# PEER down loop on one Trainium2 core: one product of 512 columns for two of 256, sums in eight banks

## What is computed

```
h   = gelu(tokens @ u.T)              # a value for each token and each expert
G   = summed softmax weights of the picked experts, 0 elsewhere
out = (h * G) @ v                     # 16384 experts, D = 1024
x   = x + gate * out
```

## Time and profile before

| | us |
|---|---|
| median of 3 runs | 4567.59 |
| lowest and highest run | 4564.38, 4571.7 |
| profiled execution, its own time | 4573.89 |
| profiled execution, span of its instructions | 4571.8 |
| TensorE busy | 4217.0 (92%) |
| TensorE weight loads busy | 3981.0 (87%) |
| VectorE busy | 3068.6 (67%) |
| ScalarE busy | 1813.9 (40%) |

### The profile page before, as it was taken

One profiled execution on the slowest core, in us unless ns is written; L12 is line 12 of the kernel. 1 busy time (PEld: TensorE's weight loads), 2 busy tenths in 40 slices (PEclk: granted clock), 3 DMA queues, 4 the chain that ended last, 5 costly groups with the idle time before them and its releaser, 6 DMA issues. The chain is left out here.

```text
span 4571.8 us, 87598 instructions
## 1 busy us (share of the span) xinstructions
PE 4217.0 (92%) x33409; PEld 3981.0 (87%) x33418; DVE 3068.6 (67%) x5237; ACT 1813.9 (40%) x2655; POOL 37.9 (1%) x54
## 2 busy tenths in 40 slices
PE   8978999969888589999999899999988889999998
PEld 8956999859784489899999898999987589899998
DVE  5565565555523648887777598877772659887777
ACT  4324343333322434444333444443332444444333
POOL 0000000000000001000000010000000001000000
PEclk9988999989899899999999999999999999999999
DMA  6633666526420037555776575567752157556775
GB/s 233 203 118 108 228 201 230 165 75 227 152 94 19 29 124 229 181 177 184 228 227 215 162 228 171 175 195 229 227 169 76 38 161 228 170 176 195 228 226 180
DMA packets 300374, 786.60 MB, mean 172 GB/s; under 512 B 32848, under 2 KB 132176, under 8 KB 299344
## 3 DMA queue, kind: packets, MB, share of 16 engines
q1 hardware_dynamic: 300112, 782.95, 54.1%
HBM read 731.44 MB, written 51.38 MB: 171 GB/s over the span
## 5 line engine op out<-in xcount | busy, mean ns | idle before, releaser
L265 PE MATMUL banks<-h_parts,ring_hi 128*128 128x256 f32 x7920 | 1981.2, 288 | 113.7 <-ACT ring_hi L248 104.8
L248 ACT ACTIVATE ring_hi<-ring 128x1024 fp32r<-128x1024 f32 x1166 | 1234.3, 1059 | 1960.1 <-PE banks L269 1931.3
L266 PE MATMUL banks<-h_parts,ring_hi 128*128 128x256 f32 x7920 | 1958.0, 284 | 0.0
L254 DVE TENSOR_TENSOR ring_lo<-ring,ring_hi 128x1024 fp32r<-128x1024 f32 x1166 | 1428.2, 1226 | 731.4 <-ACT ring_hi L248 718.5
L265 PEld LDWEIGHTS banks<-h_parts,ring_hi 128*128 128x128 f32 x7920 | 1530.9, 193 | 128.6 <-issue 66.8
L266 PEld LDWEIGHTS banks<-h_parts,ring_hi 128*128 128x128 f32 x7920 | 1532.4, 193 | 0.3
L269 PE MATMUL banks<-h_parts,ring_lo 128*128 128x256 f32 x7920 | 1116.0, 284 | 0.9 <-DVE ring_lo L254 0.6
L269 PEld LDWEIGHTS banks<-h_parts,ring_lo 128*128 128x128 f32 x7920 | 1026.2, 193 | 2.5 <-DVE ring_lo L254 2.5
L1632 DVE TENSOR_TENSOR scratch<-con,picks 128x1024 f32<-128x1024 f32 x192 | 235.3, 1225 | 128.0 <-PE banks L1516 128.0
L265 PE MATMUL banks<-h_parts_ctx,ring_hi 128*128 128x256 f32 x992 | 245.1, 285 | 0.0
L266 PE MATMUL banks<-h_parts_ctx,ring_hi 128*128 128x256 f32 x992 | 243.1, 283 | 0.0
(11 more groups left out here) (205 smaller groups left out, 3211.8 us busy)
## 6 DMA issues: line engine op xcount, KB each, us to landing
ring<-peer_u_dram SPq DMA_DIRECT2D x384, 512.0 KB, 4.0
ring<-peer_v_dram SPq DMA_DIRECT2D x384, 512.0 KB, 3.8
act_store<-acts_out SPq DMA_DIRECT2D x384, 128.0 KB, 3.2
scratch<-act_store SPq DMA_DIRECT2D x384, 128.0 KB, 3.5
ring<-ffn_gate_dram SPq DMA_DIRECT2D x88, 512.0 KB, 3.7
ring<-ffn_up_dram SPq DMA_DIRECT2D x88, 512.0 KB, 3.6
ring<-ffn_down_dram SPq DMA_DIRECT2D x88, 512.0 KB, 3.6
big<-mod_w_dram SPq DMA_DIRECT2D x80, 512.0 KB, 4.5
```

The lines of the kernel that those rows point to most:

```text
L248: self.nc.scalar.activation(self.hi[:, n % 2], self.ring[:, self.slot(j)], ACT.Copy).then_inc(self.count("tile_hi").sem, 1)
L254: self.nc.vector.tensor_tensor(self.lo[:, self.slot(j)], self.ring[:, self.slot(j)], self.hi[:, n % 2].bitcast(F32), ALU.subtract).then_in ...
L265: self.nc.tensor.matmul(out, w, b_hi, start=opens and m == 0, stop=False)
L266: self.nc.tensor.matmul(out, w, b_lo, start=False, stop=False)
```

## The change

In the down loop, the two products of a chunk that use the same high half of the weights (L265 and L266) become one: its moving operand is `h[:, 0:2, r % 2]`, the high half and the rest of the values, 2 x 256 columns, and its output is a whole bank of 512 columns. The third product stays, 256 columns, and goes into the first half of the bank. Each chunk so has a bank of its own, eight banks in all. Its sum is first half plus second half. What follows from that:
- `fall` calls `two` and no longer `three`.
- Banks 0 to 3, 6 and 7 are opened before the last up tile, and banks 4 and 5, in which the up loop makes its sums, behind it, after TensorE has waited for the last gelu.
- The last tile goes chunk by chunk (`two_by_chunk`), after waits for both halves of its weights, and signals each chunk; the closing products are gone. `tile_done` is not raised for it, and `done.ends(-1)` takes that into account.
- VectorE adds both halves of each bank into the stream, sixteen additions: first half of chunk c when it is complete, then the second half of chunk c - 1.

The up loop, the ring, the splitting and all other layers stay.

```diff
+    def two(self, pe, j, turns, terms, b_hi, b_both):
+        hi, lo = self.count("tile_hi"), self.count("tile_lo")
+        pe.wait_ge(hi.sem, turns * RING + hi.after(j + 1))
+        for out, c in terms:
+            self.nc.tensor.matmul(out, self.hi[:, j % 2, c * P:(c + 1) * P], b_both, start=False, stop=False)
+        pe.wait_ge(lo.sem, turns * RING + lo.after(j + 1))
+        for out, c in terms:
+            ins = self.nc.tensor.matmul(out[:, 0:T], self.lo[:, self.slot(j), c * P:(c + 1) * P], b_hi, start=False, stop=False)
+        return ins
+
+    def two_by_chunk(self, pe, j, terms, b_hi, b_both, summed):
+        hi, lo = self.count("tile_hi"), self.count("tile_lo")
+        pe.wait_ge(hi.sem, hi.after(j + 1))
+        pe.wait_ge(lo.sem, lo.after(j + 1))
+        for out, c in terms:
+            self.nc.tensor.matmul(out, self.hi[:, j % 2, c * P:(c + 1) * P], b_both, start=False, stop=False)
+            self.nc.tensor.matmul(out[:, 0:T], self.lo[:, self.slot(j), c * P:(c + 1) * P], b_hi, start=False,
+                                  stop=True).then_inc(summed.sem, 1)
...
-    acc = k.ps[:, 0:4].rearrange("p b (c t) -> p (b c) t", t=T)
+    falls = [(k.ps[:, c], c) for c in (0, 1, 2, 3, 6, 7, 4, 5)]
...
                 pe.wait_ge(ready.sem, i * R + ready.after(r + 1))
-                k.three(pe, N + r, i, [(acc[:, c], c, h[:, 0, r % 2], h[:, 1, r % 2]) for c in range(KD)],
-                        False).then_inc(done.sem, 1)
+                k.two(pe, N + r, i, falls, h[:, 0, r % 2], h[:, 0:2, r % 2]).then_inc(done.sem, 1)
...
                     pe.wait_ge(kept.sem, kept.after(STEPS))
-                    k.open_banks(range(4))
+                    k.open_banks((0, 1, 2, 3, 6, 7))
                 rise(e)
...
+            pe.wait_ge(acted.sem, acted.after(N))
+            k.open_banks((4, 5))
             with pe.Fori(0, turns) as i:
                 for r in range(R):
                     fall(r, i)
-            for r in range(R):
+            for r in range(R - 1):
                 fall(r, turns)
-            k.close_banks(range(4)).then_inc(summed.sem, 1)
+            pe.wait_ge(ready.sem, ready.after(N))
+            k.two_by_chunk(pe, 2 * N - 1, sorted(falls, key=lambda f: f[1]), h[:, 0, 1], h[:, 0:2, 1], summed)
...
+            def other(c):
+                dve.wait_ge(added.sem, added.after(c + 1))
+                nc.vector.scalar_tensor_tensor(stream[:, c], k.ps[:, c, T:2 * T], gate[:, c:c + 1], stream[:, c], ALU.mult, ALU.add)
...
-            dve.wait_ge(summed.sem, summed.after(1))
             for c in range(KD):
-                nc.vector.scalar_tensor_tensor(stream[:, c], acc[:, c], gate[:, c:c + 1], stream[:, c], ALU.mult, ALU.add)
+                dve.wait_ge(summed.sem, summed.after(c + 1))
+                nc.vector.scalar_tensor_tensor(stream[:, c], k.ps[:, c, 0:T], gate[:, c:c + 1], stream[:, c], ALU.mult,
+                                               ALU.add).then_inc(added.sem, 1)
+                if c:
+                    other(c - 1)
+            other(KD - 1)
```

More of the change, by code:

```diff
@@ L118 @@
     "top_step", "pair_scores", "first_keys_marked", "pick_step", "weight_exp", "picks_turned", "keys_marked", "marks_weighted", "gate_product", "gate_kept",
-    "gelu_done", "expert_weighted", "picks_kept", "mod_product", "mod_product_kept", "mod_turned", "mod_kept", "lam_copied", "lam_products", "lam_dots", "lam_exps", "lam_ready",
+    "gelu_done", "expert_weighted", "half_added", "picks_kept", "mod_product", "mod_product_kept", "mod_turned", "mod_kept", "lam_copied", "lam_products", "lam_dots", "lam_exps", "lam_ready",
 )
@@ L1465, in experts @@
     marked, marks_weighted, product, kept = map(k.count, ("keys_marked", "marks_weighted", "gate_product", "gate_kept"))
-    weighted, rounded, ready, summed = map(k.count, ("expert_weighted", "hidden_hi", "hidden_ready", "sums_complete"))
+    weighted, rounded, ready, summed, added = map(k.count, ("expert_weighted", "hidden_hi", "hidden_ready", "sums_complete",
+                                                            "half_added"))
     both_halves = sv.rearrange("p (n two) b -> p n two b", two=2)
@@ L1741, in experts @@
     picked.ends(3)
-    summed.ends(1)
+    summed.ends(KD)
+    added.ends(KD)
     k.ring_ends(2 * N)
+    done.ends(-1)
 def prepare(k):
```

## The result

| us | before | after |
|---|---|---|
| median of the runs | 4567.73 (4564.38 to 4571.7, 6 runs) | 4533.08 (4529.46 to 4540.71, 6 runs) |
| profiled execution, its own time | 4573.89 | 4540.71 |

The ratio is 0.9924 (95% interval 0.9911 to 0.9937): 34.7 us less, where the forecast said 75.5.

The account below looks back on a forecast made before the run. TensorE's product starts were taken to bound the down loop, 2.88 us a tile. Tiles gaining 74.7 us and ends 0.8 gave 75.5 us less, 4492 as the median, range 4485 to 4570.

Parts of the forecast that it names:

- The price of a product of 512 columns: Down loop, high half: one wide product costs 215.5 ns where two narrow ones cost 240, saving 196 ns a tile.
- It is something that takes about 120 ns of wall time beside the product: Down loop's fp32r products: the 12 ns extra at 256 columns is covered once a product lasts 213 ns.
- a part of the extra stays with every product: Rival, down loop: a weight load steals 12 ns from each product, 227.5 ns, 38 us won, 4529; chance 0.25.
- The argument against the limit: A feed-forward tile of the same form took 118.8 ns a product, so 120 is no hard limit of the stream.
- The stream is the limit: Rival, down loop: 512 fp32r columns cost 240 ns, so TensorE saves nothing, 4566 to 4570; chance 0.17.
- slower than 240: Rival, down loop: two separate runs or two passes push the wide product over 240 ns, at most 5150; chance 0.08.
- The others keep up: Down loop: VectorE's chain of 2.66 us, ScalarE and transfers meet the 2.68 us tile, VectorE narrowly; no cost.
- The openings and the new wait: Before the down loop: 0.43 us of openings hidden in TensorE's pause; gelu wait costs 0, at most 0.5 a loop.
- The end: Last down tile: start to last addition 6.91 us instead of 7.18, gaining 0.3 us a loop, 0.8 in all.

Follow-up runs that it names:

- The bf16 runs: Kernel after with bf16 constants as weights and moving values in steady down tiles: wide products only, 4496.83 us; all 24 products at 256 columns, 4472.43 us.
- Starts and ends alone: Kernel after with each 512-column product made as two of 256 again, eight banks, openings and sixteen additions kept: 4567.72 us, ratio 0.9995 to the kernel before.
- the kinds in turn: Kernel after with one 512-column and one 256-column product per bank alternating through each down tile: 4542.2 us, ratio 0.9946 to the kernel before.

## Why the prediction was wrong

The forecast was 4492; measured 4533.08, inside the range of 4485 to 4570.

- **The price of a product of 512 columns** is the step that failed: 215.5 ns in the sum, 230 measured. It stood on bf16 and plain f32 rows of the same width, taken as "the row of the same width and one pass". The bf16 runs show that this price is nearly right for bf16 in this very place (217), and the fp32r runs that it is not fp32r's: 113.3 ns for 256 columns at best and so 226.7 for 512, plus some 3 ns on average. 3048 x 14.5 ns = 44.2 us less gained, and 381 x 7 ns = 2.7 us more from the low ones, which the sum did not have: 41.5 us, and 75.5 - 34.7 is 40.8.
- **"It is something that takes about 120 ns of wall time beside the product"** was the wrong conclusion from the low clock. 213.8 ns at 1.2 GHz left no room for a fixed extra behind each product there, and I took it to exclude a cost that grows with the columns at full clock as well. But a limit in columns per nanosecond (256 in 113.3) is hidden at half the clock in the same way, and it does grow with the columns. The forecast named such a limit as a rival only at 256 in 120, which would have left no gain.
- **The rival "a part of the extra stays with every product"** gave 227.5 ns and 4529 us, 4 us off. Its number was right and its mechanism wrong: it had the weight load steal a fixed 12 ns, and 32 columns of weights in place of 128 leave the wide product at 230. Of the 11 ns that separate 120 from bf16's 109, 4 are there at the best fp32r rate too (113.3 - 109) and 6.7 come and go.
- **The argument against the limit**, the feed-forward tile of 118.8 ns a product, did show that 120 is no floor. It said nothing on a floor at 113.3, and I read it as leave to go down to 108.
- **"The stream is the limit" at 240, and slower than 240**: neither came. One run of 512 columns in place of two changes nothing.
- **The others keep up**: right. PE is busy without a gap at 2.79 us, and with bf16 at 2.69 the kernel still came to 4496.83. The forecast's "met, narrowly" was too careful: bf16 tiles ran at 2.62 us without a wait of PE, under the 2.66 us of VectorE's chain.
- **The openings and the new wait**: right in mechanism. With the 0.43 us added, the way to the first fall is 0.49 us longer in the first loop, 0.24 shorter in the second and 0.15 longer in the third: 0.4 us lost in all, where the forecast had 0 and at most 0.5 a loop. The load for which the fall waits does not move with the openings; its own scatter (2.71 to 3.47 us from issue to use) is what is left.
- **The end**: right, 6.92 against 6.91 us, some 0.3 us won a loop. Starts and ends alone gave a ratio of 0.9995 (0.9985 to 1.0004), which agrees with a net of next to nothing.
- **The account**: 33.1 us from the tiles and some 0.4 from starts and ends (0.8 - 0.4). The medians say 34.7 and the profiled executions 33.2, which is within the runs' scatter.

The Trainium skill ("TensorE: Matmul & The Clock Gate", section "Back-to-back issue gap") gives N/2.4 + 2.5 ns between isolated products of N columns at the full clock and names no type: by this page an estimate of 216 ns for 512 columns and 109 for 256. The bf16 runs here agree (217 and 109), though each product has a weight load beside it; for such a stream the same section of the Trainium skill has about 131 ns at 512 columns, which no run here shows. The fp32r runs don't agree (230, and 113 to 120). The measurement decides.

## What to carry to other kernels

Price a product by rows of its own data type; a row of the same width in another type is a bound and not the value, even where both make one pass. A limit per nanosecond and a fixed cost beside each product look the same at one width and at a lower clock, and part only when the width changes; so keep both as cases with their prices. The cheapest way to part them beforehand is a stretch in which two widths of the same type run at the full clock. Check a pace over a whole loop as well: one tile at the fast pace (347 ns a pair) did not show that the pace lasts.

## What the runs showed of the hardware

- At the full clock an fp32r product of 256 columns takes 113.3 ns at best (2.26 columns a nanosecond) and a bf16 one 109; at 512 columns it is 230 against 217. At the lower clock fp32r has 213.8 for 256 columns, with no such excess.
- Beyond that fp32r products lose up to about 6.7 ns each on average, in patterns that can hold for tens of tiles. Over 24 x 113.3 = 2.72 us (or 8 x (226.7 + 113.3), the same), the tile of the kernel before has 0.16 (24 x 6.7), 96 columns of weights leave 0.06, 64 columns 0.16 in one loop and 0 in two, and the kernel after has 0.07 with 16 products. So what merging products saved is this part only, down from 0.16 to 0.07 us.
- The same instructions can run at two paces (119.9 or 113.3 ns a product; 2.77 or 2.83 us a tile with the kinds in turn), taken up at a loop's start or changed in its course. That the width of the weights matters is seen (115 against 119 for the low ones after the change), and that cutting the weights' transfer, copy and subtraction to an eighth leaves the tile at 2.79; how a loop comes into the slow or the fast pace is open.
